# Gates three ahead, compressed attention in five pieces, norm sums four side by side, output in eight

## What is computed

```python
# first block
a  = (rms_norm(o_hg) * silu(g_hg)) @ w_branch_a
bb = o_att @ w_branch_b
y  = (sigmoid(ga) * a + sigmoid(gb) * bb) @ w_out
x  = x + g1 * y
x  = x + g2 * expert_choice_moe(modulate(rms_norm(x, norm2_g), sh2, sc2), ...)  # 16 experts, 64 tokens each
x  = rms_norm(x, final_norm_g)
# second block
h  = rms_norm_2(x, g_mix_norm); z = h @ w_in
# per query block: compressed keys, selected keys, window keys
p_cmp = masked_softmax(s - slopes * dist, dist >= 0)      # 31 compressed keys, 8 heads
o  = gates[0] * o_cmp + gates[1] * o_slc + gates[2] * o_win
x  = x + concat(rms_norm_2(attn_out), rms_norm_2(conv_out)) @ w_o
h  = rms_norm_2(x, g_ffn_norm)
x  = x + square(relu(h @ w_up)) @ w_down
```

## Time and profile before

| | us |
|---|---|
| median of 3 runs | 1953.2 |
| lowest, highest | 1952.46, 1954.58 |
| the profiled execution | 1954.31 |
| its span | 1953.0 |
| PE busy in it | 1750.6 (90%) |
| DVE busy | 796.8 (41%) |
| ACT busy | 568.7 (29%) |
| GpSimd busy | 123.1 (6%) |
| TensorE's clock, mean | 0.955 |

### The profile page before, as it was taken

How to read it: one execution, slowest core, us unless ns; L and a number is a source line. 1 busy time by engine, 2 the same in 40 slices (tenths; PEclk the granted TensorE clock), 3 DMA queues, 4 the chain that set the end, 5 groups by cost and what they waited for, 6 DMA issues and landing times.

```text
span 1953.0 us, 20332 instructions
## 1 busy us (share of the span) xinstructions
PE 1750.6 (90%) x8144; PEld 1136.5 (58%) x8144; DVE 796.8 (41%) x1322; ACT 568.7 (29%) x1023; POOL 123.1 (6%) x127
## 2 busy tenths in 40 slices
PE   5999899887999896999888888999888999999998
PEld 2656567565877673333333233687544678888786
DVE  2164654457534332111111102437566534444443
ACT  2224553564333331110110000431544442222221
POOL 0002121012000001000000000000100101101100
PEclk9999799888999897999999999999988899999999
DMA  8221201123413447999999999243300122223201
GB/s 304 93 67 43 87 22 44 65 87 130 122 51 131 184 157 283 424 424 424 423 424 425 423 424 410 79 128 91 125 1 1 44 86 87 87 86 114 103 1 43
DMA packets 92562, 329.40 MB, mean 169 GB/s; under 512 B 7717, under 2 KB 22709, under 8 KB 67893
## 3 DMA queue, kind: packets, MB, share of 16 engines
q1 hardware_dynamic: 85408, 315.80, 41.7%
q10 hardware_dynamic: 5716, 8.05, 1.3%
q0 software_dynamic: 1344, 4.25, 0.6%
HBM read 322.83 MB, written 4.20 MB: 167 GB/s over the span
## 4 chain that ended last, share of the span: by engine, by line
PE 70%; DMA 10%; DVE 10%; ACT 6%; issue 3%; ACTq 0%; SPq 0%; DVEq 0%
PE PS L665 21%; PE PS L808 11%; PE PS L1038 9%; PE PS L408 7%; DMA room<-in_w_exp_gate_dram 7%; PE PS L404 3%; PE PS L539 3%; PE PS L621 3%; PE PS L819 3%; PE PS L873 2%; PE PS L464 1%; DMA room<-in_w_exp_down_dram 1%; DMA ring<-in_w_in_dram 1%; PE PS L686 1%; PE PS L988 1%
## 5 line engine op out<-in xcount | busy, mean ns | idle before, releaser
L1754 DVE TENSOR_TENSOR wR<-ring,wR 128x1024 fp32r<-128x1024 f32 (+2 forms) x134 | 151.4, 1130 | 237.8 <-ACT wR L1150 237.7
L1150 ACT CAST wR<-ring 128x1024 fp32r<-128x1024 f32 (+2 forms) x134 | 130.0, 971 | 211.8 <-PE PS L1038 128.1
L1038 PE MATMUL PS<-wR,hR 128*128 128x512 f32 x768 | 177.8, 393 | 8.9 <-DVE tmp L2506 6.9
L665 PE MATMUL PS<-xR,wR 128*128 128x512 f32 x768 | 175.6, 389 | 0.0
L1038 PEld LDWEIGHTS PS<-wR,hR 128*128 128x128 f32 x768 | 144.7, 189 | 42.0 <-DVE tmp L2506 9.6
L665 PEld LDWEIGHTS PS<-xR,wR 128*128 128x128 f32 x768 | 144.0, 188 | 30.3 <-issue 0.4
L665 PE MATMUL PS<-hR,wR 128*128 128x512 f32 x528 | 130.3, 405 | 7.9 <-DVE hR L2487 3.3
L808 PE MATMUL PS<-ring,xeT 128*64 128x512 f32 x512 | 116.2, 604 | 10.2 <-DMA ring<-in_w_exp_gate_dram 9.2
L808 PE MATMUL PS<-room,xeT 128*64 128x512 f32 x512 | 114.0, 593 | 11.4 <-DMA room<-in_w_exp_gate_dram 11.4
L665 PEld LDWEIGHTS PS<-hR,wR 128*128 128x128 f32 x528 | 100.8, 193 | 35.8 <-issue 9.3
L665 PE MATMUL PS<-hR1h,wR 128*128 128x512 f32 x320 | 104.6, 401 | 8.5 <-DVE hR1m L2151 7.5
(11 more groups left out here) (451 smaller groups left out, 2699.1 us busy)
## 6 DMA issues: line engine op xcount, KB each, us to landing
ring<-in_w_exp_gate_dram SPq DMA_DIRECT2D x32, 1024.0 KB, 25.5
room<-in_w_exp_gate_dram SPq DMA_DIRECT2D x32, 1024.0 KB, 26.0
ring<-in_w_exp_up_dram SPq DMA_DIRECT2D x32, 1024.0 KB, 26.2
room<-in_w_exp_up_dram SPq DMA_DIRECT2D x32, 1024.0 KB, 25.9
ring<-in_w_exp_down_dram SPq DMA_DIRECT2D x32, 1024.0 KB, 26.2
room<-in_w_exp_down_dram SPq DMA_DIRECT2D x32, 1024.0 KB, 27.7
ring<-in_w_mod_dram SPq DMA_DIRECT2D x12, 2048.0 KB, 7.8
ring<-in_w_in_dram SPq DMA_DIRECT2D x11, 2048.0 KB, 8.5
```

The costliest lines, as they stand in the source:

```text
L665: mm = T.matmul(b, o[s][:, k, :], x(t, k), start=(k == ks[0] and j == 0), stop=(k == ks[-1] and j == 2))
L1038: mm = T.matmul(down[m], uR[:, r % 2, s, k, 128 * i:128 * i + 128], o[t][:, 0, 512 * q:512 * q + 512], start=(k + j == 0), stop=(k == 3 an ...
L1150: A.copy(parts(wR, chunks, n)[0], W.view(unit)[:, ks, cs]).then_inc(act_hi.sem, act_hi.up(key))
L1754: V.tensor_tensor(lo, W.view(unit)[:, ks, cs], hi.bitcast(F32), ALU.subtract) \
```

## The change

Five edits.

1. Mix, second branch: `mg` runs three ahead of `wb` (mg0, mg1, mg2, then wb t, mg t+3). The sigmoids go to four places (`sqs`) in place of two; `turn_x` is one step earlier; the high copies of `uT` are spread over wb 5 to 7 (five, one, two) and the low parts likewise (three, two, three); PE waits for them k by k in the first wo tile.
2. Scatter 7 and the second block's norm: squares of four tiles in four places, added up four side by side in 32 rows each (`shares`), once inside the scatter behind k = 5 and once inside raw 0 before its k = 4; DVE copies the totals to `sq`, and two full matmuls with ones close them behind raw 0. The weights of raw 0 are split inside the scatter (`copy_hi` at k = 3, `sub_lo` at k = 4). The second block's places in `wR` are swapped. `cN` is turned behind raw 1, and the eight products of `xT` come behind raw 1 too. `PT` is made before the wait for the down product, and PE's scatter waits for `ye`.
3. Selection: the compressed branch in five pieces at m = 3, 4, 5, 7, 8 for i = 3 and 9, 10, 11, 13, 14 (then every eight) for the others. The end of the stage (`drain`, m = 32 and 33) makes the conv tiles' high and low parts, splits the first wo2 weights, and takes the norm of blocks 1 to 3 with Ln and Exp; products by the norm move from GpSimd to DVE.
4. wo2: squares four side by side (`total3`), once behind tile 5 and once inside the turned tiles, and one closing matmul `sum3`.
5. The output goes in eight transfers of 256 KB, each behind its own add.

```diff
     for t in range(8):
-        mix_chunks += mg[1][t:t + 1] + wb[1][t:t + 1]
+        mix_chunks += wb[1][t:t + 1] + mg[1][t + 3:t + 4]
...
+        at = (n + (chunks is not mix_chunks)) % 2
+        return [wR[:, at, x, 0:a * b].rearrange("p (a b) -> p a b", b=b) for x in range(2)]
...
-        def squares(b, mats, k, nk, sig, key):
-            for dst, m in zip(b, mats):
-                mm = T.matmul(dst, m, sq[:, k % 2, :], start=(k == 0), stop=(k == nk - 1))
-            mm.then_inc(sig.sem, sig.up(key))
+        def shares(totals, mats, tiles, n, ready, result):
+
+            sem, key = result
+            T.wait_ge(*ready[4 * n + 3])
+            for total, mat in zip(totals, mats):
+                for k in range(4 * n, 4 * n + 4):
+                    r = 32 * (k % 4)
+                    mm = T.matmul(total[r:r + 32, :], mat(k), tiles[k % 4], start=(n == 0), stop=(n == 1))
+            mm.then_inc(sem.sem, sem.up(key))
...
                 for k in range(8):
                     b = pool.take(T, ("sc", p, k), dve_moe["x", p, k])
-                    T.wait_ge(*dve_moe["PT", p])
+                    T.wait_ge(*dve_moe["ye", p, 1])
...
-                    if total and k:
-                        T.wait_ge(*act_moe["sq", k - 1])
-                        squares(total, [ones, gmat[:, k - 1, :]], k - 1, 8, pe_moe, ("sq", k - 1))
+                    if total and k == 5:
+                        total2(0)
...
                     if v == 0:
+                        for i in range(2):
+                            b = pool.take(T, ("sum2", i), (act_sec["lnr"], dve_sec["total"])[i])
+                            T.wait_ge(*dve_moe["share", i])
+                            T.matmul(b, ones, sq[:, i, :], start=True, stop=True).then_inc(pe_sec.sem, pe_sec.up(("sum2", i)))
...
-            if m < 32 and m % 8 == (3 if m < 8 else 1):
-                compressed1(sel_steps[m][0])
-            if m < 32 and m % 8 == (6 if m < 8 else 5):
-                compressed2(sel_steps[m][0])
+            for n, step in enumerate((c_scores, c_exp, c_norm, c_turn, c_put)):
+                at = (3, 4, 5, 7, 8)[n], (9, 10, 11, 13, 14)[n]
+                if m == at[0] or m >= at[1] and (m - at[1]) % 8 == 0 and m < 32:
+                    step(3 if m == at[0] else 3 - m // 8)
+            if m in (32, 33):
+                drain(m)
...
+                    if br and t >= 5:
                         A.wait_ge(*pe_mm[("mg", 1, 7), 0])
-                        for k in range(7):
+                        for k in (range(5), (5,), (6, 7))[t - 5]:
...
+                if k == 3:
+                    A.wait_ge(*pe_moe["down", 7, 3])
+                    copy_hi(wR2, sec_chunks, 0)
...
+            def drain(m):
+
+                if m == 32:
+                    A.wait_ge(*pe_sel["s", 31])
+                    A.wait_ge(*dve_sel["conv"])
+                    conv_hi((4, 5))
+                    A.wait_ge(*pe_sel["pT", 29, 1])
+                    copy_hi(wR3, ffn_chunks, 0)
+                else:
+                    conv_hi((6, 7))
+                    A.wait_ge(*dve_sel["tot", 1])
+                    A.activation(rinv[:, 128:512], rinv[:, 128:512], ACT.Ln).then_inc(s.sem, s.up())
+                    A.wait_ge(*s.last)
+                    A.activation(rinv[:, 128:512], rinv[:, 128:512], ACT.Exp, scale=-0.5).then_inc(s.sem, s.up("rinv1"))
...
         for b in range(8):
+            i, q = b // 2, b % 2
             S.wait_ge(*dve_ffn["xo", 7, b])
-        S.dma_start(out.rearrange("(i p) n -> p i n", p=128),
-                    mixT.rearrange("p (i q) n -> p i (q n)", q=2)).then_inc(s_out, 16)
-        S.wait_ge(s_out, 16)
+            S.dma_start(out[128 * i:128 * i + 128, 512 * q:512 * q + 512], xo[:, i, q, :]).then_inc(s_out, 16)
+        S.wait_ge(s_out, 16 * 8)
```

More of the change, by code:

```diff
@@ L661, in chunk_tile @@
             for k in ks:
+                if between and k == 4:
+                    between()
                 if ready:
@@ L699, in half @@
             mm.then_inc(pe_mix.sem, pe_mix.up(("logits", n)))
-            T.wait_ge(*act_mix["sqy", 4 * n + 3])
-            for k in range(4 * n, 4 * n + 4):
-                r = 32 * (k % 4)
-                mm = T.matmul(total[r:r + 32, :], ones[:, 0:32], sqs[k % 4], start=(n == 0), stop=(n == 1))
-            mm.then_inc(pe_mix.sem, pe_mix.up(("sums", n)))
+            shares([total], [lambda k: ones[:, 0:32]], sqs, n, {4 * n + 3: act_mix["sqy", 4 * n + 3]}, (pe_mix, ("sums", n)))
         def turn_rows(pool, i, q):
@@ L841, in experts, with total2 @@
             pool = Banks(6, 8)
-            total = [pool.take(T, ("total2", i), (act_sec["lnr"], dve_sec["total"])[i]) for i in range(2)]
+            for i in range(2):
+                pool.take(T, ("total2", i), dve_moe["share", i])
             T.wait_ge(*pool_moe["gmat"])
-            scatter(7, total)
-            T.wait_ge(*act_moe["sq", 7])
-            squares(total, [ones, gmat[:, 7, :]], 7, 8, pe_moe, ("sq", 7))
+            scatter(7, True)
+        def total2(n):
+            shares([bank(("total2", i)) for i in range(2)], [lambda k: ones[:, 0:32], lambda k: gmat[:, k, 0:32]],
+                   squares2, n, {4 * n + 3: act_moe["sq", 4 * n + 3]}, (pe_moe, ("sums", n)))
         def second():
@@ L993, in square2 @@
             def square2(i):
[L994 removed]
+                b = pool.take(T, ("tot2", i), dve_sel["tot", i] if i else act_sel["rms2", 0])
                 T.wait_ge(*act_sel["sqa", i])
@@ L1019, in ffn @@
                             for q in range(2):
+                                if (i, q) == (1, 0):
+                                    total3(total, 1)
+                                if (i, q) == (2, 1):
+                                    b = pool.take(T, "sum3", act_ffn["rinv"])
+                                    T.wait_ge(*dve_ffn["share"])
+                                    T.matmul(b, ones, tmp[:, 2, :], start=True, stop=True) \
+                                        .then_inc(pe_ffn.sem, pe_ffn.up("sum3"))
                                 b = pool.take(T, ("xo", i, q), act_ffn["xo", i, q])
@@ L2122, in after @@
                     br, t = key[1:]
-                    if br and t == 7:
-                        for k in range(7):
-                            V.wait_ge(*act_mix["uR", k])
-                            V.tensor_tensor(hR1(1, k), uT[:, k, :], hR1(0, k).bitcast(F32), ALU.subtract) \
-                                .then_inc(s.sem, s.up(("uR", k)))
+                    if br and 5 <= t < 7:
+                        low((range(3), range(3, 5))[t - 5])
                     V.wait_ge(*pe_mm[key, 0])
                     V.wait_ge(*act_mix["mg", br, t])
-                    b, g = bank(key)[:, 0:512], sg[:, t % 2, :] if br else uT[:, 4 + t % 4, :]
+                    b, g = bank(key)[:, 0:512], sqs[t % 4] if br else uT[:, 4 + t % 4, :]
                     if br == 0:
@@ L2498, in ffn @@
                     if t == 7:
+                        V.wait_ge(*pe_ffn["sums", 1])
+                        V.tensor_copy(tmp[:, 2, :], bank("total3")[:, 0:512]).then_inc(s.sem, s.up("share"))
                         V.wait_ge(*act_ffn["rinv"])
```

200 lines of the change are left out of this document (106 added, 94 removed).

## The result

| | before | changed |
|---|---|---|
| median, us | 1952.8 (4 runs) | 1931.1 (4 runs) |
| lowest to highest | 1949.3 to 1954.6 | 1928.2 to 1934.5 |
| ratio (95% interval) | | 0.9892 (0.987 to 0.9914) |
| the profiled execution; its span | 1954.31; 1953.0 | 1930.07; 1928.8 |

The change saves 21.7 us. The forecast was 1924.8 with a range of 1915 to 1934: right in sign and range, 6.3 us too fast, and at the very edge of the narrower span of 1920 to 1931 that had the largest chance. In two lines of the changed kernel's page TensorE (PE) is still busy for 90% of the span, 16 us less than before, and there is still a dip of the granted clock in some slices.

What follows compares the result with a forecast made beforehand. PE stalls and the half clock behind many of them were taken as the bound, with transfers setting the experts' stage. Terms -8.65 + 3.4 - 14.5 - 4.3 - 4.3 = -28.35 on a 1953.2 median gave 1924.8, range 1915 to 1934.

Steps and rivals of the forecast that it cites:

- Mix: Mix before the experts: PE's 7.5 us wait before wo0 mostly goes and 120 matmuls run at full clock; -8.65 us.
- rival (b): Experts' stage absorbs the mix's gain because its transfers are not tied to PE's arrival; 1933.5 us, chance 0.04.
- Scatter and entry: Scatter 7 and entry to the second block: new PE idles, half clock and a later kv wait cost +3.4 us.
- the third case: Entry to second block: slow shares and slow raw0 too, second kv chunk at 47.0 us after the last down product; +3.4.
- Selection: Selection up to wo2: PE's waits for the compressed softmax go, part returns as waits for scaled p; -14.5 us.
- wo2: wo2 tiles: 0.86 us saved a tile for six tiles, less one group of shares; -4.3 us.
- Unchanged code: Conv products and start of the selection, between kw products and first scores: no change predicted, 0 us.
- Output: After the last DVE add: eight transfers, the last 256 KB landing in 2.1 us against 6.4 for the whole; -4.3 us.
- rival (e): Output: the eight writes run one after another, each its own 5.0 us; 1957.8 us, chance 0.02.
- (d): Clock stays at half over the whole entry to the second block and first wo2 tiles; +10 more, 1935, chance 0.06.
- (a): Selection blocks 3 to 1: DVE becomes the bound, its 3.2 us a block return, clock stays down; 1933.3, chance 0.12.
- (c): The scatter costs nothing and wo2's entry is at full clock; 1917.9 us, chance 0.15.

Runs made afterwards that it cites:

- e2_mix_back: Changed kernel with the mix edit undone: gates one ahead again, high copies behind the last branch tile, PE waiting for all; 1939.5 us, ratio 0.9935.
- e3_scatter_back: Changed kernel with the scatter 7 and second-block norm edit undone, only the earlier PT kept; 1925.0 us, ratio 0.9864.
- e5_fill: Changed kernel with five repeated matmuls added in scatter 7, in PE's idle before the first shares; 1925.6 us, ratio 0.9856.
- e1_sums4: Changed kernel with wo2's shares of the first four squares run behind tile 4 in place of tile 5; 1924.8 us, ratio 0.9869.
- e7_out_one: Changed kernel with the output in one 2 MB transfer again; 1939.2 us, measured a single time.
- e8: Changed kernel with scatter 7 laid out anew: DVE adds before low parts, eight square places, later shares, raw 0 in bank 2, its weights earlier; 1916.7 us, ratio 0.9811.
- e9_products: Changed kernel with DVE's eight xT products moved from behind raw 1 to behind the second and third kv chunks' low weights; 1928.9 us, ratio 0.9886.
- e10_all: Changed kernel with four edits together: wo2 shares earlier, cpT copy first, scatter and entry laid out anew, xT products moved; 1898.6 us, ratio 0.9725.

## Why the prediction was right, and where it was not

**Mix (-8.65, measured -8.9): right,** step by step: PE waits 0.17 before wb7 (0.2 said), 0.76 before wo0 (0.95) and 0.95 at the second mg1 tile (0.9), and the clock stayed up. The same code took 202.8 to 204.8 in ten kernels, so the gain is 8.9 to 10.8. That the experts pass it on (and rival (b) fell) is shown by e2_mix_back.

**Scatter and entry (+3.4, measured +3.1): right,** and for the reason given: two idles, half clock behind both, a later wait before kv. e3_scatter_back takes it back; e5_fill shows the clock's part at the shares alone. That 3.1 fell so close to 3.4 is partly luck: by the six kernels with this code the cost on before is 1.7 to 4.2. The price of an idle was read from rows with shorter ones, and "the third case" was the one that came.

**Selection (-14.5, measured -15.7): right in sum, less so in its parts.** Blocks 3, 2 and 1 gave 3.4, 3.7 and 1.8 (4.3, 3.8, 1.6 forecast). Block 0 and the way to wo2 gave 6.8 for 4.8. The walk had the square of o0 3.5 us behind PE's last value; it came 0.5 behind it, and PE idled 1.9 us in front of the first wo2 matmuls in place of 4.1. What I missed is that a bank is a queue too: with the copy of `cpT` a step behind the turn, the next turn waits for it, 4.6 us. And the size holds only for this execution: the same code took 128.7 to 135.3 in eight kernels (changed, e1, e2, e3, e5, e7, e8, e9), so the gain on the one trace of before is 10 to 17. The bounds of -10 and -18.5 held.

The table loads were counted rightly by the rows. ACT's timeline of the changed kernel, in front of the last square:

```profile
1500.22 1.28 ACT L1665 ACT_TABLE_LOAD   x1
...
1502.05 1.28 ACT L1667 ACT_TABLE_LOAD   x1
```

L1665 is the Ln, L1667 the Exp. The Trainium skill (ScalarE: Activation LUTs, section Table sets: the hidden batching unit) has both in one set, which would make one load. Here the trace differs, and there are two, as in the earlier trace rows.

**wo2 (-4.3, measured +1.3): wrong,** and the one step that failed. The forecast took 0.86 us a tile from the full matmuls and costed the rest at nothing. But the change also added a wait, of ACT's fifth square for PE's shares, and the text did not say what was queued behind it: the high copy of the weights of tile 6. With ACT late by the length of a tile, PE stood 3.71 us and then ran at half clock. e1_sums4 removes the wait and finds the -4.1. The same wait in the scatter had been walked through (there it was 1.55 us); in wo2 it had not.

**Unchanged code (0, measured +3.2): missed.** Between the kw products and the first scores both kernels have the same work and the same stall of 1.9 us, with 168 matmuls behind it that take 38.33 and 39.96. PE's timelines of before, 1304 to 1380, and of the changed kernel, 1294 to 1366:

```profile
1334.28 38.33 PE L665 MATMUL PS<-hR,wR 128*128 128x512 f32 x168 [1.89 <-DVE wR L1754]
```

```profile
1324.88 39.96 PE L671 MATMUL PS<-hR,wR 128*128 128x512 f32 x168 [1.91 <-DVE wR L1790]
```

The stretch by windows, for before, for the changed kernel and for e2_mix_back:

```profile
1304.77:1388.70 83.93, 79.34 (x384) 62.00 (x383) 57.70 (x82) 24.66 (x37) 5.21 (x8) 1.00 0.31 88
```

```profile
1295.36:1382.49 87.13, 82.40 (x385) 63.89 (x384) 57.69 (x82) 24.67 (x37) 5.22 (x8) 0.96 0.30 84
```

```profile
1302.80:1386.77 83.97, 79.25 (x385) 62.01 (x384) 57.71 (x82) 24.68 (x38) 5.22 (x8) 1.00 0.30 87
```

The 3.2 us are PE's busy time at a lower clock. Half of them lie in these 168 matmuls. The other half stand behind a wait of 2.6 to 2.7 us for a square, where the next eight matmuls took 3.80 before and 5.37 in the changed kernel. The 3.2 are there with the scatter undone (e3_scatter_back, 87.15) and not with the mix undone, so the scatter's edit is not their cause. Whether the order of the mix is, hundreds of us earlier, or only when PE's work arrives there, these runs don't settle. The code alone doesn't fix it: e7_out_one, the same up to the output, took 88.5, and e9_products and e10_all lie between (85.5).

**Output (-4.3, measured -4.5): right;** rival (e) fell, and e7_out_one gives the 4.5 back. The estimate from the Trainium skill (DMA: Bandwidth & Descriptors, sections Anatomy of one DMA and Bandwidth) was -4.2, from a fit that the page made on transfers issued by GpSimd. The ones here, issued by SyncE, landed after 6.4 and 2.0 us where it gives 6.8 and 2.6. Here its wish for large batches cost nothing to ignore, as the eight overlap with the adds.

**The sum.** Leaving out the unchanged start, -21.2 was measured for -28.35. Of the 7.1 between, wo2 is 5.6 and unchanged stretches 4.0 (3.2, 0.6, 0.2); the experts, the selection, the mix, the entry and the output gave back 2.5. So one failed term and one stretch whose time was taken as fixed both made the kernel slower than forecast, and the total stayed in the range only because it left 9 us of room on that side. The rivals: (b), (d) and (e) did not come; of (a) the waits for scaled p came, but not the low clock; of (c), wo2's entry at full clock came (12 matmuls in 3.02 us, 6.35), the free scatter did not.

## What to carry to other kernels

For every wait that a change adds, write down what stands behind it in that engine's queue and who needs that; a place given back two tiles later can cost more than the work it saves. Where two engines hand a tile back and forth, let the first start the next tile before it finishes this one, and see first that the third engine has room for the faster pace: here the layout that does this was worth 12.7 us, and it rests on the cheaper squares. Compare two kernels stretch by stretch, with busy time and granted clock apart, or the clock's part will be taken for that of the edit. Look also at how much an unchanged stretch differs between kernels that share its code, before you put a us down to an edit.

## What the runs showed of the hardware

The clock's share surprised me. The selection with the same instructions took 128.7 us at a mean clock of 0.92 and 135.3 at 0.86, and the one with more idle of PE (19.1 us against 18.3) was the faster. Five matmuls that compute nothing, put into an idle of 5.4 us, made the next eight twice as fast (3.6 to 1.85 us) and paid 1.7 us. And the start of the program, the same in all kernels, ended between 535.3 and 542.4 us, so a difference of 3 us between two profiled executions says nothing until it is put down to a stretch.
